# Norms computed inside the expert stages, and the last four experts handled one at a time

## The reference, cut to what matters

```python
for l in range(DEPTH):
    h = rmsnorm_2(x, norm1_g[l]) * (1.0 + sc1) + sh1
    ...
    x = x + g1 * (merged @ w_out[l])
    h = rmsnorm_2(x, norm2_g[l]) * (1.0 + sc2) + sh2
    x = x + g2 * peer(h, w_query[l], sub_keys[l], expert_u[l], expert_v[l])
return rmsnorm_2(x, final_g)
```

## Time and profile before

| | us |
|---|---|
| median of 3 runs | 2440.79 |
| lowest and highest run | 2440.41, 2445.68 |
| profiled execution | 2443.84 |
| its span | 2442.2 |
| PE / DVE / ACT / POOL busy | 2110.2 / 1604.5 / 791.6 / 564.8 |

### The profile page before, as it was taken

How to read it: one execution, slowest core, us unless ns; L and a number is a source line. 1 busy time by engine, 2 the same in 40 slices (tenths; PEclk the granted TensorE clock), 3 DMA queues, 4 the chain that set the end, 5 groups by cost and what they waited for, 6 DMA issues and landing times. The chain is left out here.

```text
span 2442.2 us, 24858 instructions
## 1 busy us (share of the span) xinstructions
PE 2110.2 (86%) x8748; PEld 1362.7 (56%) x8748; DVE 1604.5 (66%) x3291; ACT 791.6 (32%) x1701; POOL 564.8 (23%) x604
## 2 busy tenths in 40 slices
PE   6689989989979999998788777699998987778776
PEld 5478867778869766554333333397664543333332
DVE  6567864577865658666766775656486677667755
ACT  4444435444445623221122112255232211221111
POOL 0000010000000213333334333102033433333331
PEclk9889989999989999999899999899999998998998
DMA  7068863188854449999999999854399999999996
GB/s 278 1 251 317 296 226 112 69 309 319 305 211 173 151 177 419 421 421 421 421 421 421 421 417 422 330 179 171 126 409 422 421 421 422 421 422 421 421 421 256
DMA packets 161332, 773.24 MB, mean 317 GB/s; under 512 B 12966, under 2 KB 13350, under 8 KB 89548
## 3 DMA queue, kind: packets, MB, share of 16 engines
q0 software_dynamic: 80640, 587.24, 58.6%
q1 hardware_dynamic: 80588, 184.69, 21.0%
HBM read 770.79 MB, written 1.10 MB: 316 GB/s over the span
## 5 line engine op out<-in xcount | busy, mean ns | idle before, releaser
L2582 ACT ACTIVATE experts_diagonal<-ident,experts_weight 128x128 f32<-128x128 f32 x508 | 162.4, 390 | 662.3 <-DVE experts_weight L2471 657.5
L2690 PE MATMUL experts_fourth<-ring,experts_diagonal 128*128 128x512 f32 x448 | 214.9, 629 | 53.7 <-ACT experts_diagonal L2582 53.7
L2246 POOL DMA_INDIRECT ring<-in_experts_uv_dram,experts_at x196 | 186.2, 950 | 309.2 <-PE experts_fourth L2690 144.4
L187 DVE TENSOR_TENSOR mix_lo<-ring,mix_hi 128x1024 fp32r<-128x1024 f32 x96 | 132.1, 1383 | 118.7 <-ACT mix_hi L1954 118.7
L2447 DVE CUSTOM_DVE_ANT_0 ring<-ring,experts_second 128x1024 f32<-128x1024 f32 x116 | 141.5, 1220 | 99.7 <-DMA ring<-in_experts_uv_dram,experts_at 98.9
L2246 POOL DMA_INDIRECT experts_v_slot<-in_experts_uv_dram,experts_at x160 | 154.4, 965 | 211.1 <-PE experts_fourth L2690 111.2
L2690 PE MATMUL experts_fourth<-experts_v_slot,experts_diagonal 128*128 128x512 f32 x320 | 157.7, 634 | 38.0 <-ACT experts_diagonal L2582 38.0
L2690 PEld LDWEIGHTS experts_fourth<-ring,experts_diagonal 128*128 128x128 f32 x448 | 87.4, 200 | 178.5 <-issue 102.3
L2690 PE MATMUL experts_first<-ring,experts_diagonal 128*128 128x512 f32 x320 | 155.7, 636 | 34.5 <-ACT experts_diagonal L2582 34.5
L2690 PE MATMUL experts_first<-experts_v_slot,experts_diagonal 128*128 128x512 f32 x320 | 152.2, 616 | 15.4 <-ACT experts_diagonal L2582 15.4
L192 PE MATMUL mlp_hid<-mix_hT_hi,mlp_in_hi 128*128 128x256 f32 x512 | 147.2, 288 | 5.9 <-DVE mlp_in_lo L187 5.9
(11 more groups left out here) (463 smaller groups left out, 4968.7 us busy)
## 6 DMA issues: line engine op xcount, KB each, us to landing
mlp_ada_rows<-in_ada_turned_dram POOLq DMA_DIRECT2D x48, 1024.0 KB, 5.4
ring<-in_w_in_dram SPq DMA_DIRECT2D x20, 2048.0 KB, 8.6
ring<-in_mlp_w_in_dram SPq DMA_DIRECT2D x16, 2048.0 KB, 9.9
ring<-in_mlp_w_out_dram SPq DMA_DIRECT2D x16, 2048.0 KB, 9.9
ring<-in_gla_w_in_dram SPq DMA_DIRECT2D x6, 2048.0 KB, 7.9
ring<-in_w_query_dram SPq DMA_DIRECT2D x6, 2048.0 KB, 8.5
ring<-in_w_out_dram SPq DMA_DIRECT2D x4, 2048.0 KB, 8.0
ring<-in_attn_w_qkv_dram SPq DMA_DIRECT2D x3, 2048.0 KB, 11.8
```

Source lines behind the costliest of these rows:

```text
L187: return dve.tensor_tensor(out_lo, a, hi.bitcast(F32), ALU.subtract)
L2246: pool.indirect_dma_start(pair(i), None, rows, bass.IndirectOffsetOnAxis(ap=at[:, n, j:j + 1], axis=0)).then_inc(pair_in[slot_of(i)], 16)
L2582: act.activation(diagonal[:, i % TOPK, :], K.ident[:], ACT.Copy, scale=weight[:, n, i % TOPK:i % TOPK + 1]).then_inc(diagonal_ready, 1)
L2690: mm = pe.matmul(y[n // PH][:, b, :], diagonal[:, j, :], v_row(i)[:, b * HALF:(b + 1) * HALF], start=n % PH == 0 and j == 0, stop=False, s ...
```

## The change

The two `norm` stages behind the expert stages are gone; `experts` does their work, and writes `hT` for the next `mix` or, in layer 1, the output. `hT` now lives through the expert stage and shares its memory with `scores`.

For tile 0, ACT squares in unit 13 and takes the root in unit 14 (each root needs its table, and gelu's again behind it), DVE scales and shifts behind dots 11 and 12 of unit 14, PE transposes in unit 14, ACT and DVE take the result out behind group 3 of unit 14 and dots 6 and 7 of unit 15. In layer 1 the final gain row is spread like the others, and tile 0's output is stored once the last pair has landed.

For tile 1, the last four experts (`SINGLES`) each get their own gelu, weight and diagonal, and all go over PE. PE reports each half of the last row (`y_halves`); DVE adds it to `K.x` by halves (`give_last`), ACT squares the halves, and scale, shift, transposes and output go by halves. The product of the gain row with its scale moves from behind unit 14 to behind unit 12. Panels 2 and 3 of layer 1's `mix` start at its own beginning.

```diff
+        start_panels(sp, K, first_panels)
...
-def experts(nc, K, A, l, shared, keysT, following=()):
+def experts(nc, K, A, l, hT, scores, shared, keysT, following=(), out=None):
...
-    BY_DVE = range(ALL - 2, ALL)
+    SINGLES = range(ALL - GROUP, ALL)
...
-scores = st.sb("scores", [P, T, PH, 2 * NKEYS])
...
+last_x = xn[:, 1, :]
+added, gained = (h2T[:, 4 * n:4 * n + 4, :].rearrange("p k n -> p (k n)") for n in range(2))
...
-if following:
+if out is not None:
+    row_sources += [A.final_g_2.rearrange("(a n) -> a n", a=1)]
+    row_targets += [K.mod[:, 0, :]]
+else:
...
+back = (first, second)
+squares = third[:].rearrange("p b n -> p (b n)")
...
+        else:
+            sp.wait_ge(pair_in[slot_of(ALL - 1)], pair_arrived(ALL - 1))
+            sp.wait_ge(last_there, 1)
+            sp.dma_start(out[0][0:P, :], last_x).then_inc(stored, 16)
+            for n in range(2):
+                sp.wait_ge(last_there, 2 + n)
+                sp.dma_start(out[0][P:S, part(n)], gained[:, part(n)]).then_inc(stored, 16)
+            sp.wait_ge(stored, 16 * 3)
...
-                if n == LAST and j in (TOPK - GROUP - 1, TOPK - 1):
+                if n == LAST and j == TOPK - GROUP - 1:
                     weigh(i // GROUP)
+                if i in SINGLES:
+                    weigh_one(i)
+                if n >= LAST - 1:
+                    normalise_first(n, j)
+        def normalise_first(n, j):
+            if (n, j) == (LAST - 1, 2):
+                dve.wait_ge(last_squared, 1)
+                dve.tensor_scalar(last_ms[:, 0:1], last_ssq[:, 0:1], 1.0 / D, EPS, ALU.mult,
+                                  ALU.add).then_inc(last_ms_done, 1)
+            elif (n, j) == (LAST - 1, 11):
+                dve.wait_ge(last_std_done, 1)
+                own(dve.reciprocal(last_rstd[:, 0:1], last_std[:, 0:1]))
+                ins = dve.scalar_tensor_tensor(out=last_x, in0=K.x[:, 0, :], scalar=last_rstd[:, 0:1],
+                                               in1=K.mod[:, 0, :], op0=ALU.mult, op1=ALU.mult)
+                if out is None:
+                    own.begun(ins)
+                else:
+                    ins.then_inc(last_there, 1)
+            elif (n, j) == (LAST - 1, 12) and out is None:
+                own.settled()
+                dve.tensor_tensor(last_x, last_x, K.mod[:, 1, :], ALU.add).then_inc(last_there, 1)
+            elif (n, j) in ((LAST, 6), (LAST, 7)) and out is None:
+                dve.wait_ge(last_hi, j - 5)
+                rest_of(dve, halves(hT.lo, j - 6), back_half(0, j - 6), halves(hT.hi, j - 6))
+        def weigh_one(i):
+            j = i % TOPK
+            dve.wait_ge(gelu_done, SINGLES.start // GROUP + i - SINGLES.start + 1)
+            dve.tensor_tensor(weight[:, LAST, j:j + 1], dots[:, LAST, j:j + 1], e[:, LAST, j:j + 1],
+                              ALU.mult).then_inc(weight_done, 1)
...
-        def give_x(t, sums_of):
-            own(dve.tensor_tensor(scaled, sums_of, factor2, ALU.mult))
-            own(dve.tensor_tensor(K.x[:, t, :], K.x[:, t, :], scaled, ALU.add))
+        def give_first():
+            dve.wait_ge(v_used, TOPK * PH)
+            dve.wait_ge(row_in, 1)
+            own(dve.tensor_tensor(scaled, y[0][:].rearrange("p b n -> p (b n)"), factor2, ALU.mult))
+            dve.tensor_tensor(K.x[:, 0, :], K.x[:, 0, :], scaled, ALU.add).then_inc(x_given, 1)
+        def give_last(n):
+            dve.wait_ge(y_halves, n + 1)
+            own(dve.tensor_tensor(added[:, part(n)], y[1][:, n, :], factor2[:, part(n)], ALU.mult))
+            dve.tensor_tensor(K.x[:, 1, part(n)], K.x[:, 1, part(n)], added[:, part(n)],
+                              ALU.add).then_inc(x_given, 1)
...
-                dve.wait_ge(v_used, TOPK * PH)
-                dve.wait_ge(row_in, 1)
-                give_x(0, y[0][:].rearrange("p b n -> p (b n)"))
-        if following:
-            dve.wait_ge(row_in, ROWS)
-            own(dve.scalar_tensor_tensor(out=K.mod[:, 0, :], in0=scale1, scalar=1.0, in1=K.mod[:, 0, :],
-                                         op0=ALU.add, op1=ALU.mult))
+                give_first()
+            if n == PH + 4:
+                dve.wait_ge(row_in, ROWS)
+                if out is None:
+                    own(dve.scalar_tensor_tensor(out=K.mod[:, 0, :], in0=scale1, scalar=1.0,
+                                                 in1=K.mod[:, 0, :], op0=ALU.add, op1=ALU.mult))
         unit(LAST)
-        also = scores[:, 0, 4:PH, :].rearrange("p h n -> p (h n)")
-        dve.wait_ge(weight_done, ALL // GROUP)
-        for n, i in enumerate(BY_DVE):
-            by = weight[:, LAST, i % TOPK:i % TOPK + 1]
-            if n == 0:
-                dve.tensor_scalar(also, v_row(i), by, None, ALU.mult).then_inc(v_by_dve, 1)
+        for n in range(2):
+            give_last(n)
+        dve.wait_ge(last_squared, 2)
+        dve.tensor_scalar(last_ms[:, 1:2], last_ssq[:, 1:2], 1.0 / D, EPS, ALU.mult,
+                          ALU.add).then_inc(last_ms_done, 1)
+        dve.wait_ge(x_given, 3)
+        own.several(*(dve.tensor_tensor(gained[:, part(n)], K.x[:, 1, part(n)], K.mod[:, 0, part(n)], ALU.mult)
+                      for n in range(2)))
+        dve.wait_ge(last_std_done, 2)
+        own(dve.reciprocal(last_rstd[:, 1:2], last_std[:, 1:2]))
+        for n in range(2):
+            if out is not None:
+                dve.tensor_scalar(gained[:, part(n)], gained[:, part(n)], last_rstd[:, 1:2], None,
+                                  ALU.mult).then_inc(last_there, 1)
             else:
-                dve.wait_ge(v_by_dve, n)
-                dve.scalar_tensor_tensor(out=also, in0=v_row(i), scalar=by, in1=also, op0=ALU.mult,
-                                         op1=ALU.add).then_inc(v_by_dve, 1)
-        dve.wait_ge(v_by_dve, len(BY_DVE))
-        dve.wait_ge(v_used, ALL - len(BY_DVE))
-        own(dve.tensor_tensor(also, also, y[1][:].rearrange("p b n -> p (b n)"), ALU.add))
-        give_x(1, also)
+                dve.scalar_tensor_tensor(out=last_x[:, part(n)], in0=gained[:, part(n)],
+                                         scalar=last_rstd[:, 1:2], in1=K.mod[:, 1, part(n)], op0=ALU.mult,
+                                         op1=ALU.add).then_inc(last_there, 1)
+        for n in range(2, 4) if out is None else ():
+            dve.wait_ge(last_hi, n + 1)
+            rest_of(dve, halves(hT.lo, n), back_half(1, n - 2), halves(hT.hi, n))
...
-                    if i in BY_DVE:
-                        continue
...
+                if (n, k) == (LAST - 2, 0):
+                    act.wait_ge(x_given, 1)
+                    act.activation(squares, K.x[:, 0, :], ACT.Square,
+                                   accum_out=last_ssq[:, 0:1]).then_inc(last_squared, 1)
+                if (n, k) == (LAST - 1, 0):
+                    act.wait_ge(last_ms_done, 1)
+                    act.activation(last_std[:, 0:1], last_ms[:, 0:1], ACT.Sqrt).then_inc(last_std_done, 1)
+                if (n, k) == (LAST - 1, TOPK // GROUP - 1) and out is None:
+                    for h in range(2):
+                        take_back(0, h)
+        def take_back(t, h):
+            n = 2 * t + h
+            act.wait_ge(last_turned, n + 1)
+            act.activation(halves(hT.hi, n), back_half(t, h), ACT.Copy).then_inc(last_hi, 1)
+        def weigh_one(i):
+            j = i % TOPK
+            act.wait_ge(dots_done, i + 1)
+            act.activation(dots[:, LAST, j:j + 1], dots[:, LAST, j:j + 1],
+                           ACT.Gelu_apprx_tanh).then_inc(gelu_done, 1)
+            act.wait_ge(weight_done, SINGLES.start // GROUP + i - SINGLES.start + 1)
+            act.wait_ge(v_used, i - TOPK + 1)
+            act.activation(diagonal[:, j, :], K.ident[:], ACT.Copy,
+                           scale=weight[:, LAST, j:j + 1]).then_inc(diagonal_ready, 1)
...
+        for i in SINGLES:
+            weigh_one(i)
         act.activation(std[:, T + 1:T + 2], K.ident[:, 0:1], ACT.Sqrt)
+        for n in range(2):
+            act.wait_ge(x_given, n + 2)
+            act.activation(third[:, n, :], K.x[:, 1, part(n)], ACT.Square,
+                           accum_out=last_ssq[:, 1 + n:2 + n]).then_inc(last_squared, 1)
+        act.wait_ge(last_squared, 3)
+        act.wait_ge(last_ms_done, 2)
+        act.activation(last_std[:, 1:2], last_ssq[:, 2:3], ACT.Sqrt, scale=1.0 / D,
+                       bias=last_ms[:, 1:2]).then_inc(last_std_done, 1)
+        for h in range(2) if out is None else ():
+            take_back(1, h)
...
+                    if i == ALL - 1:
+                        mm.then_inc(y_halves, 1)
+                if i < ALL - 1:
+                    mm.then_inc(v_used, 1)
+        def turn_back(t, h, there):
+            pe.wait_ge(last_there, there)
+            for k in range(4):
+                f = (4 * h + k) * P
+                mm = pe.transpose(back[t][:, h, k * P:(k + 1) * P], last_x[:, f:f + P], K.ident[:])
```

(11 more changed lines are left out.)

54 lines of the change are left out of this document (30 added, 24 removed).

## The result

| | before | after |
|---|---|---|
| median of 5 runs each, us | 2440.79 (2439.97 to 2445.68) | 2427.41 (2427.17 to 2432.61) |
| ratio, 95% interval | 1 | 0.9942 (0.9931 to 0.9953) |
| profiled execution, us (span) | 2443.84 (2442.2) | 2427.41 (2425.8) |

The kernel became faster by 13.4 us by the medians and by 14.2 by the ratio (0.0058 x 2440.79). The forecast was 9.7 us, 2431.1, with a low end of 2427.0. So direction and place were as forecast, and the size was too small.

A forecast was written before the change was run, and what follows sets the result against it. DMA gathers at about 421 GB/s were taken to bound both expert stages, leaving only their ends to shorten: 4.6 + 5.1 = 9.7 us off 2440.79 gives 2431.1. Range 2427 to 2436.5, the forecast's own 2427.5 to 2434.5.

The forecast's parts named there:

- The ends: From the last dot to layer 0's first mixing matmul 4.6 us less, to layer 1's span end 5.1 less.
- the third rival: At both ends, hand-overs between engines cost 0.3 us more each, 5.4 us go, 2436.5 is left; chance 0.12.
- The step that rests on PE's queue: At layer 0's end, PE's backlog sets the pace: expert 252 starts at 1558.33, 255 only at 1563.49.
- the change of stage: From layer 0's expert stage to ACT's first split in mixing: 1.14 us taken, the other row being 0.81.
- a half-size last transfer: At layer 1's end, the last output transfer, half as large at 256 KB, might save 0.6 us.
- transposes at the full clock: At layer 0's end, transposes taking 1.20 us instead of 1.97 would save 0.4 to 0.8 us, 10.3 in all.
- Nothing for the added work: Inside the expert stages, added DVE, ACT and PE work costs nothing, as queued gathers cover delays under 9.4 us.
- the lead of 16.8 us: From the last gather's issue at 1540.70 to its dot at 1557.52; shortest issue to landing is 7.4 us.
- The fourth rival: In units 13 to 15 the gathers fall behind and all added work lies on the path, 2448.0; chance 0.05.
- PE without a backlog: At both ends, expert 255's matmul starts at its own diagonal, 3.8 us less in each layer, 2423.5; chance 0.05.
- PE at 1.2 GHz: In the last twelve experts PE runs partly at the lower clock, costing about 1.45 us, 2434.0 for both layers; chance 0.08.
- A rule against the trace: For PE's transposes, the skill says the full clock does not engage; the trace has 1.20 us behind matmuls, 1.97 after idle.

The follow-up runs named there:

- neither: The changed kernel with both norms again as stages and experts 254 and 255 on DVE, keeping the shared memory of hT and scores; 2439.67 us, 0.9991 of before.
- before_twice: The kernel before, unchanged, timed against itself; 2440.14 us, ratio 0.9992.
- alone12: The changed kernel with its last twelve experts one by one instead of four, weights of 240 to 243 formed behind dot 243; 2420.80 us, 0.9910 of before.
- after_third: The changed kernel as it is, a third time; 2427.63 us, 0.9942 of before.
- after_again: The changed kernel as it is, a second time; 2427.98 us, 0.9947 of before.

## Why the prediction was wrong in its size and right in its mechanism

**The ends (forecast 9.7 us, measured 10.7 at full clock).** Layer 0, in us behind the start of the last dot, forecast as in the prediction's working and measured as in the rows above:

| | forecast | measured | this step alone: forecast, measured |
|---|---|---|---|
| PE starts 252 | 0.81 | 0.81 | |
| first half of the row at DVE | 7.20 | 7.02 | |
| reciprocal | 11.52 | 11.13 | 4.32, 4.11 |
| transposes start | 12.53 | 12.13 | 1.01, 1.00 |
| last remainder ends | 15.86 | 15.26 | 3.33, 3.13 |
| ACT's first split | 17.00 | 16.19 | 1.14, 0.93 |
| first mixing matmul | 19.37 | 18.56 | 2.37, 2.37 |

Four terms were each priced 0.2 us too high, the first of them DVE's half behind PE's start of 252 (6.39 for 6.21). No step was dearer than forecast, as the third rival would have it. The step that rests on PE's queue came out exactly. Two of the four had a choice in them: for the change of stage I took the higher of two rows, 1.14 and not 0.81, and it was 0.93; for the transposes I took a row of 3.33 behind 1.97 us of transposes, and they took 1.77 here. Layer 1: forecast 16.1, measured 15.92 and 15.91, in the first execution 18.76 by the clock. The two scalings took 0.44 us each where I took 0.4, and the last stretch to the end of the span 3.71 where I took 3.55.

**What stood outside the ends (forecast 0, measured about 3 us by the ratio).** This is the step that failed. The sum "4.6 + 5.1 = 9.7" takes all that the change does not touch as fixed, a term of 0 without a reason given, and its range has nothing for it either: what the prediction names for the low side, a half-size last transfer (0.6 us) and transposes at the full clock (0.4 to 0.8), comes to about 1.4 of the 3.6 us down to its own low end, 2427.5. In its place the runs showed a surplus over the ends in each of the three comparisons (3.4, 2.1 and 3.4 us), and 1.2 to 2.2 us in neither, which has no new end. Part of it may be the reading of the ratio, which made before_twice 2.0 us faster than itself; the repeats speak against chance alone, and the cause stays open. The ends add 1 us to the miss. In the first pair of profiled executions the shares are different again: 16.4 us less in all, 7.8 of it in the two ends (the lower clock took 2.8 back) and 8.6 elsewhere, 4.3 of these before the first dot.

**Nothing for the added work: right.** The reason fits too: the dots keep their pace (637.3, 636.9 and 637.3 us for 255 dots in layer 0 after, 639.6, 637.8 and 637.3 before), and the gathers' median is the same. How large a delay the lead of 16.8 us would cover was not tried. The fourth rival, the only one on the slower side, did not occur anywhere.

**The rivals.** PE without a backlog did not occur, and alone12 shows its price, 3.5 and 3.7 us for each layer against 3.8 worked out. PE at 1.2 GHz occurred among the last 16 experts in both layers of the first execution, in both of after_third and in layer 0 of after_again, but only once from expert 244 on, where it counts. There it was dearer than worked out, 2.84 for 1.45. The stretch of before that I took for its length and price (0.71 over 5 us) belongs to the group of 240 to 243, which has idle time behind it with and without the change (1.89 us in before), so it showed neither the place nor the length of the drop that costs something. The spans do not show it, 2425.8 us with it and 2425.6 without, as the scatter elsewhere is as large.

**A rule against the trace.** Eight transposes took 1.04 us in unit 14, right behind matmuls, and 1.77 at the end, behind 4.29 us without work. The first row:

```profile
1516.74 1.04 PE L2807 MATMUL experts_first<-ident,experts_xn 128*128 128x128 f32 x8
```

By these rows what the transposes take follows from what PE did before. The Trainium skill's sentence (TensorE: Matmul & The Clock Gate, Part 4: PE-mode transpose), that the full clock does not engage for transposes, is not what these rows show: the granted clock from 1516.7 to 1517.8 is 1.00. Whether transposes alone would bring the clock up is not shown here. The 0.4 to 0.8 us that the full clock would have given at the end did not come, for the transposes stand behind idle time there; they took 1.77 us, 0.2 less than the row that the sum used, at a granted clock of 0.66 over the 2 us from 1562.9. ACT's root follows its table load at 0.01 us in unit 14 (1489.55 + 1.28 to 1490.84), as before the change, so the drain that the Trainium skill (ScalarE: Activation LUTs, What ACT_TABLE_LOAD costs) adds does not appear here either.

## What to carry to other kernels

A stage that one resource paces has its only cheap time at its end, and what counts there is the queue of the engine that finishes: before refining the last items, look whether that engine starts them without idle time, and if it does, feed it earlier. Here the groups of four further ahead, not the last four, held back the end, and alone12 took another 6 to 7 us by forming their diagonals as soon as their dots were there. A forecast of some tenths of a per cent needs a term, or room in its range, for what the change leaves alone, also where every other term of its sum is known to 0.2 us. Timing the old kernel against itself (here 0.9992) helps to tell how large that room must be.
